# Four phase heads with only what is first needed in front, and prompt scores as two products of stacked halves, in a two-layer streaming encoder step

## What is computed

```
layer 0:  h = x @ w_in            -> MLA (latent attention, 8 heads) || retention (8 heads)
layer 1:  h = x @ w_in            -> GLA (gated linear attention)    || SWA (windowed softmax attention)
both:     x = LayerNorm(a*x + concat(parts) @ w_out);  x = LayerNorm(a*x + ConvFFN(x))

SWA, per query row of the prompt: 8 query heads in 2 groups over 2 key/value heads of size 64,
  s = q . k * 64**-0.5   over its own chunk of 64 rows and the 128 rows before it, masked elsewhere
  o = softmax([s, sink]) @ v
MLA for a stream: s = (q_abs . cached latent + q_pe . cached rotary key) * scale over 1024 cached rows
```

## Time and profile before

| | |
|---|---|
| median of 3 runs | 3093.89 us (3088.95 to 3095.7) |
| profiled execution, its own time | 3095.32 us |
| its span, first to last instruction | 3093.5 us |
| PE (TensorE) busy | 2939.1 us, 95% of the span |
| PE weight loads | 2612.2 us, 84% |
| DVE, ACT, POOL busy | 1648.3, 1056.4, 827.4 us: 53%, 34%, 27% |
| mean granted TensorE clock | 0.976 |
| instructions | 42586 |

### The profile page before, as it was taken

The page is one execution under the profiler, slowest core; times in us unless marked ns, Lnnn a source line. Parts: engine busy times, 40 slices in busy tenths (PEclk is TensorE's granted clock), DMA queues, the critical chain, the costliest instruction groups (busy, mean ns, idle before and its releaser), DMA issues. The chain is left out here.

```text
span 3093.5 us, 42586 instructions
## 1 busy us (share of the span) xinstructions
PE 2939.1 (95%) x15775; PEld 2612.2 (84%) x15775; DVE 1648.3 (53%) x2648; ACT 1056.4 (34%) x2087; POOL 827.4 (27%) x699
## 2 busy tenths in 40 slices
PE   8899789998999999999997998998999999999997
PEld 7455678886899999999996898996899999999996
DVE  3566635656545555555547442445455555555556
ACT  5334532333432322222333453333332232222323
POOL 1245211112232322222335000102233322222324
PEclk9999899999999999999998998998999999999998
DMA  3100531103111111111103101113111111111112
GB/s 126 34 8 13 180 117 35 35 22 128 46 55 41 41 45 43 41 41 41 41 28 107 47 5 40 39 35 121 35 60 41 41 47 41 47 41 41 41 35 80
DMA packets 72712, 162.57 MB, mean 53 GB/s; under 512 B 19514, under 2 KB 33995, under 8 KB 71540
## 3 DMA queue, kind: packets, MB, share of 16 engines
q1 hardware_dynamic: 72596, 161.00, 16.3%
HBM read 146.51 MB, written 15.11 MB: 52 GB/s over the span
## 5 line engine op out<-in xcount | busy, mean ns | idle before, releaser
L135 PE MATMUL psum<-xT_hi,tk_whi 128*128 128x384 f32 x2112 | 711.7, 337 | 7.5 <-ACT tk_u L2317 3.3
L136 PE MATMUL psum<-xT_lo,tk_whi 128*128 128x384 f32 x2112 | 710.5, 336 | 0.0
L137 PE MATMUL psum<-xT_hi,tk_wlo 128*128 128x384 f32 x2112 | 710.3, 336 | 0.0
L2516 DVE TENSOR_TENSOR x_or_mix<-x_or_mix,psum 128x512 f32<-128x512 f32 x684 | 465.9, 687 | 243.2 <-PE psum L137 242.8
L135 PEld LDWEIGHTS psum<-xT_hi,tk_whi 128*128 128x128 f32 x2112 | 397.5, 188 | 11.4 <-ACT tk_u L2320 6.1
L136 PEld LDWEIGHTS psum<-xT_lo,tk_whi 128*128 128x128 f32 x2112 | 397.5, 188 | 1.5
L137 PEld LDWEIGHTS psum<-xT_hi,tk_wlo 128*128 128x128 f32 x2112 | 397.6, 188 | 0.0
L2479 DVE SCALAR_TENSOR_TENSOR tk_c<-tk_u,tk_cw,tk_c 128x1168 f32<-128x1168 f32 x84 | 157.8, 1878 | 447.3 <-ACT tk_c L2328 447.3
L135 PE MATMUL psum<-tk_dhi,tk_gh 128*128 128x512 f32 x756 | 294.7, 390 | 1.7 <-ACT tk_u L2320 1.7
L137 PE MATMUL psum<-tk_dhi,tk_gl 128*128 128x512 f32 x756 | 295.0, 390 | 0.0
L136 PE MATMUL psum<-tk_dlo,tk_gh 128*128 128x512 f32 x756 | 294.9, 390 | 0.0
(11 more groups left out here) (395 smaller groups left out, 5475.2 us busy)
## 6 DMA issues: line engine op xcount, KB each, us to landing
tk_wraw<-in_w_up SPq DMA_DIRECT2D x88, 512.0 KB, 3.6
tk_draw<-in_w_down SPq DMA_DIRECT2D x44, 512.0 KB, 3.6
s_ckv<-in_c_ckv SPq DMA_DIRECT2D x8, 1024.0 KB, 6.2
retw_raw<-in_w_ret SPq DMA_DIRECT2D x32, 256.0 KB, 3.5
tk_mix_wraw<-in_w_out SPq DMA_DIRECT2D x16, 512.0 KB, 4.2
glaw_raw<-in_w_gla SPq DMA_DIRECT2D x32, 192.0 KB, 3.2
x_or_mix<-in_xT SPq DMA_DIRECT2D x9, 512.0 KB, 10.2
tk_xin<-in_x_in SPq DMA_DIRECT2D x9, 512.0 KB, 3.5
```

Of the source, the lines that this page charges most:

```text
L135: nc.tensor.matmul(out, a[0], b[0], start=first, stop=False)
L136: nc.tensor.matmul(out, a[0], b[1], start=False, stop=False)
L137: return nc.tensor.matmul(out, a[1], b[0], start=False, stop=last)
L2516: nc.vector.tensor_tensor(x, x, PS[:, down_bank(n), :], ALU.add).then_inc(ad, 1)
```

## The change

Five places, all in the order of work or in the form of operands; the results and all big products stay.

1. **MLA samples, stream 0.** ACT rounds pieces 0 and 1 first, then the queries, then the rotary keys, then pieces 2 and 3. DVE does the queries, pieces 0 and 1, the low halves of the queries, pieces 2 and 3, and the own mask last.
2. **Linear phases.** PE no longer waits for POOL's memsets at its start (at slot 2 now), ACT only for the one of the values; the others are cleared later. In retention POOL makes the low half of chunk 2 first and clears the values behind it. ACT runs Silu on one column first, so that the table is loaded there.
3. **SWA scores.** Operands of 128 rows in fp32r: Q1 holds the high half of q twice, K1 the high half of k over its low half; Q2 holds the low half of q over mask rows, K2 the high half of k over mask rows. Q1.K1 + Q2.K2 makes the scores of a head. They live in columns of `x_or_mix` that nothing uses then (`swa_halves`). ACT makes four copies of q instead of two and two of k instead of one; DVE makes the low halves (`halves_lo`), PE waits for them; POOL clears a staging buffer; SP loads mask rows twice more.
4. **SWA order.** In a slot with one step and a projection (`shared`), PE leaves the last two k chunks of the projection until the scores are issued; ACT's copy of v and DVE's rotation of that tile move behind.
5. **Mix head.** In layer 0 the as-is half of tile 0 no longer waits for the transposes. In both layers the high half of chunk 4 comes before `finish_stats`.

```diff
# MLA samples, ACT and DVE
+            act.wait_ge(kl[0], came(0, 0))
+            pieces_hi(0, PIECES[:2])
             q_hi(0, 0)
-            keys_hi(0, 0)
+            kpe_hi(0)
+            pieces_hi(0, PIECES[2:])
...
+            queries(0, 0)
+            keys_lo(0, 0, (0, 1))
+            queries_lo(0, 0)
+            keys_lo(0, 0, (2, 3))
             dve.wait_ge(ol_, 16)
             own_mask(0)
-            queries(0, 0)
-            queries_lo(0, 0)
-            keys_lo(0, 0)
# linear phases: SP, POOL, PE, ACT
-            sp.wait_ge(qz, 1)
+            sp.wait_ge(qz, 2)
...
-            nc.gpsimd.memset(S0[:], 0.0)
-            nc.gpsimd.memset(vz[:], 0.0)
+            if ret:
+                w.make_lo(pool, nc.gpsimd, 0, 0, (2,))
+            nc.gpsimd.memset(vz[:], 0.0).then_inc(vzd, 1)
+            if ret:
+                w.make_lo(pool, nc.gpsimd, 0, 0, range(4, KD, 2))
             nc.gpsimd.memset(QK[:], 0.0)
             if not ret:
                 nc.gpsimd.memset(Sc[:], 0.0)
             nc.gpsimd.memset(Qm[:], 0.0).then_inc(qz, 1)
-            if ret:
-                w.make_lo(pool, nc.gpsimd, 0, 0, range(2, KD, 2))
+            nc.gpsimd.memset(S0[:], 0.0).then_inc(qz, 1)
...
-            pe.wait_ge(qz, 1)
...
+                if s == 2:
+                    pe.wait_ge(qz, 2)
...
-            act.wait_ge(qz, 1)
             if ret:
                 make_hi(0, range(G.raw, KD))
+            act.wait_ge(wz, 1)
+            nc.scalar.activation(warm[:], warm[:], ACT.Silu)
+            act.wait_ge(vzd, 1)
# SWA: SP, POOL, PE, ACT, DVE
+            sp.wait_ge(on, 2)
+            sp.dma_start(Pb[HD:HD + 8, 0, :], A["swa_q_rows"][:, 0:1024]).then_inc(rwl, 16)
+            sp.dma_start(Pb[HD:HD + 8, 1, :], A["swa_k_rows"][:, 0:1024]).then_inc(rwl, 16)
...
+            nc.gpsimd.memset(Pb[:], 0.0).then_inc(on, 1)
...
+                    if n >= 2:
+                        pe.wait_ge(qkl, tiles_to(n - 1))
...
-                        keys = KT[0:HD + 4, max(t - 1, 0) * P:(t + 1) * P]
-                        last = nc.tensor.matmul(o[:, 0:P] if t == 0 else o, QT[0:HD + 4, slot(t), h, :], keys, start=True, stop=True,
-                                                skip_group_check=True)
+                        nc.tensor.matmul(o, Q1[:, *q], K1[:, near], start=True, stop=False, skip_group_check=True)
+                        last = nc.tensor.matmul(o, Q2[:, *q], K2[:, near], start=False, stop=True, skip_group_check=True)
...
-                    project(s, range(KD))
+                    project(s, range(KD - 2 if shared(s) else KD))
...
+                if rest is not None:
+                    project(rest, range(KD - 2, KD))
                 if m:
                     values(m - 1, n)
...
-                        nc.scalar.activation(QT[0:HD, slot(t), odd::2, :], src.rearrange("p (q n) -> p q n", q=2), ACT.Copy)
+                        for copy in range(2):
+                            nc.scalar.activation(Q1[64 * copy:64 * copy + 64, slot(t), :, odd, :], src.rearrange("p (q n) -> p q n", q=2), ACT.Copy)
...
+            def halves_lo(n):
+                i, t = where(n)
+                dve.wait_ge(qkT, n + 1)
+                for odd in range(2):
+                    own = slice(64 * odd, 64 * odd + 64)
+                    nc.vector.tensor_tensor(Q2[0:HD, slot(t), :, odd, :], PS[own, 2, 0:2 * P].rearrange("p (q n) -> p q n", q=2),
+                                            Q1[own, slot(t), :, odd, :].bitcast(F), ALU.subtract)
+                nc.vector.tensor_tensor(K1[HD:P, t, :], PS[0:64, 2, 2 * P:3 * P], K1[0:HD, t, :].bitcast(F), ALU.subtract).then_inc(qkl, 1)
...
+                if rest is not None:
+                    rotate(rest)
+                    if rest == TP:
+                        make_lo(1, (5, 7))
...
+                if 2 <= s <= TILES and where(s - 1)[1] != TP:
+                    halves_lo(s - 1)
# mix head: ACT (DVE's mix_lo likewise, with the waits asis and mh)
             def mix_hi(t):
-                act.wait_ge(mt, t + 1)
+                if t:
+                    act.wait_ge(mt, t + 1)
                 if AS_IS:
-                    nc.scalar.activation(xTh[:, 0:AS_IS, tile(t)], by_k(XM[:, t, 0:AS_IS * P]), ACT.Copy)
+                    last = nc.scalar.activation(xTh[:, 0:AS_IS, tile(t)], by_k(XM[:, t, 0:AS_IS * P]), ACT.Copy)
+                    if t == 0:
+                        last.then_inc(asis, 1)
+                if t == 0:
+                    act.wait_ge(mt, 1)
...
             m.make_hi(act, 3)
+            m.make_hi(act, 4)
             L.finish_stats()
-            m.make_hi(act, 4)
```

More of the change, by code:

```diff
@@ L813, in _, with pieces_hi, kpe_hi @@
         def _(act):
+            def pieces_hi(s, pieces):
+                for i in pieces:
+                    nc.scalar.activation(cacheH[s][i], cacheT[s][i], ACT.Copy).then_inc(chi, 1)
+            def kpe_hi(s):
+                nc.scalar.activation(k3[s], kraw[s][0:96, 0:PAST], ACT.Copy).then_inc(khi, 1)
             def keys_hi(b, s):
                 act.wait_ge(kl[s], came(b, s))
-                for i in PIECES:
-                    nc.scalar.activation(cacheH[s][i], cacheT[s][i], ACT.Copy).then_inc(chi, 1)
-                nc.scalar.activation(k3[s], kraw[s][0:96, 0:PAST], ACT.Copy).then_inc(khi, 1)
+                pieces_hi(s, PIECES)
+                kpe_hi(s)
             def q_hi(b, s):
@@ L868, in queries_lo, with keys_lo @@
                 nc.vector.tensor_tensor(q3[64:96, s], qpb[64:96, s, :], q3[64:96, s].bitcast(F), ALU.subtract).then_inc(qsp, 1)
-            def keys_lo(b, s):
-                for n, i in enumerate(PIECES):
+            def keys_lo(b, s, which=range(4)):
+                for n in which:
+                    i = PIECES[n]
                     dve.wait_ge(chi, 4 * b + n + 1)
@@ L1315, in _ @@
             out.norm_late = norm_late
+            nc.vector.memset(warm[:], 0.0).then_inc(wz, 1)
             nc.vector.memset(S[:, 0, :], 0.0).then_inc(sr, 1)
@@ L1380, in phase_swa @@
     (lg, lgk, ln, gt, su, suk, dsu, ach) = (c.sem("gate_" + s) for s in names)
+    qkl, rwl, rwr = (c.sem("swa_" + s) for s in ("qkT_lo", "rows_loaded", "rows_rounded"))
+    XMR = c.rounded("swa_halves", "x_or_mix", [P, NT, D])
+    K1, K2 = XMR[:, 0:TP, 0:P], XMR[:, 0:TP, P:2 * P]
+    Q1, Q2 = (XMR[:, 4 * x:4 * x + 4, 2 * P:4 * P].rearrange("p (s a) (b n) -> p s a b n", s=2, n=P) for x in range(2))
     SCALE = HD ** -0.5
@@ L1386, in phase_swa @@
     SLOTS = UNITS + 1
+    shared = lambda s: s < TILES and len(STEPS.get(s, ())) == 1
     where = lambda n: (n // NT, ORDER[n % NT])
@@ L1552, in values, with step @@
                 last.then_inc(pv, 1)
-            def step(m, n=None):
+            def step(m, n=None, rest=None):
                 if m:
@@ L1617, in _ @@
                 if steps:
-                    step(steps[-1], s - 3 if 3 <= s < 3 + NT else None)
+                    step(steps[-1], s - 3 if 3 <= s < 3 + NT else None, s if shared(s) else None)
                 if s == TILES:
@@ L1670, in step @@
                     nc.scalar.activation(PTs[:, (m - 1) % 2, 4:4 + nb, :], PS[:, 7, 0:nb * P].rearrange("p (b n) -> p b n", n=P), ACT.Copy).then_inc(pta, 1)
+                if rest is not None:
+                    keep_v(rest)
+                    if rest == TP:
+                        make_hi(1, range(4, KD))
                 if m < UNITS:
@@ L1705, in _ @@
                     make_hi(1, range(4))
-                if s < TILES:
+                if s < TILES and not shared(s):
                     keep_v(s)
@@ L1709, in _ @@
                     keep_qkT(s - 1)
-                if s == TP:
-                    make_hi(1, range(4, KD))
                 if steps:
-                    step(steps[-1])
+                    step(steps[-1], s if shared(s) else None)
                 gate(s)
@@ L1816, in _ @@
                     make_lo(1, (1, 3))
-                if s < TILES:
+                if s < TILES and not shared(s):
                     rotate(s)
-                if s == TP:
-                    make_lo(1, (5, 7))
                 if steps:
-                    step(steps[-1], s - 3 if 3 <= s < 3 + NT else None)
+                    step(steps[-1], s - 3 if 3 <= s < 3 + NT else None, s if shared(s) else None)
+                if 2 <= s <= TILES and where(s - 1)[1] != TP:
+                    halves_lo(s - 1)
                 if s == 15:
```

37 lines of the change are left out of this document (33 added, 4 removed).

## The result

The changed kernel takes 3070.0 us (median of 4 runs, 3066.4 to 3071.4) against 3094.2 before (4 runs): a ratio of 0.992, interval 0.9906 to 0.9934. In a later session it took 3070.2 against 3094.2, ratio 0.9922 (0.9909 to 0.9936). The forecast was 3070. The sum held. Of the terms under it one failed in kind, as the experiments show, and one in size, so that the exact hit is in part luck.

The account below looks back on a forecast made before the run. PE was taken as the bound, busy 2939.1 of 3093.5 us, with losses at phase heads, in SWA and in slow clock behind waits. Terms summed to -24.9 us from 3095.3, giving 3070 us; 8-in-10 range 3058 to 3082.

Parts of the forecast that it names:

- Part 1: MLA samples: ACT's pieces go before the queries, so PE starts earlier; -1.8 us, gain between 0 and 2.8.
- Part 2: Retention head: PE starts without POOL's memsets and chunk 6 comes sooner; -4.0 us, ends -2.5 and -5.5.
- the end that it gave to a shorter slow stretch: Retention head: -5.5 us if the clock falls less because the idle before PE's start shrinks.
- Part 3: GLA head: table loaded while POOL clears the values, PE starts at 1910.6; -3.1 us, ends -2.0 and -4.5.
- the 1.19 us from ACT to PE: GLA head: rest of the 2.47 us between ACT's and PE's starts after the table load, kept for the new start.
- Part 4: SWA scores stacked in fp32r: 0.78 us a unit, -10.9 us; +0.7 for one-tile units, +0.25 for the phase's head.
- The step of 0.122 us: SWA scores: time per fp32r matmul of 256 columns, from a line through wider products; upper end 0.176.
- The added work hides beside PE: SWA slots: extra ACT copies and DVE's `halves_lo` cost nothing; without that cover a slot pays up to 1.1 us.
- rival F: SWA gets a new ring of waits through PE, ACT and DVE, making the kernel slower: 3105 us, chance 0.02.
- Part 5: SWA order: no stall for DVE's weights copy at the seam, -5.0 us; shorter wait near the end, -1.
- Part 6: Mix heads: PE's wait for chunk 4 goes, POOL delays DVE's norm chain; -0.4 us layer 0, +0.4 layer 1.

Follow-up runs that it names:

- run 1: The changed kernel with the stacked SWA scores but the old order in a slot: 3089.0 us against 3091.0, ratio 0.9993.
- run 2: The kernel before with the new SWA order alone, scores in float32 as they were: 3082.8 us against 3091.0, ratio 0.9973.
- run 3: The changed kernel with the SWA phase of the kernel before: 3084.2 us against 3094.7, ratio 0.9964.
- run 10: The changed kernel, DVE making all mix low halves, GLA's norm-weight wait moved to first use, `halves_lo` before writing out in SWA's last two slots: 3051.7 us against 3094.2.

## Why the prediction was right, and where not

- **Part 1, samples, -1.8.** Right: -2.0 by the means of nine executions, 2.4 in the pair with fewer loads. DVE's piece did take 2.44 us beside POOL.
- **Part 2, retention, -4.0.** Right: -4.3 between the two profiles and -5.5 by the means, the end that it gave to a shorter slow stretch; the start and chunk 6 come earlier as it said.
- **Part 3, GLA, -3.1.** Mis-sized: -1.5. The step that failed is the 1.19 us from ACT to PE, taken from a head in which DVE's own wait for norm weights was already over. PE starts 3.4 to 4.2 us into the phase instead of the 2.8 of the step; with that wait away it starts at 2.2, and the phase gains 4.1, part of it by the clock.
- **Part 4, scores.** The step of 0.122 us was right (0.12), and so was 0.75 a unit in the steady slots. "The added work hides beside PE" failed in kind. It was argued from busy shares, 4.03 of 10.11 us for ACT; but it is not the share that matters, it is ACT's place in the chain transposes, q and k, attention weights, values. I had put the price of losing that cover at up to 1.1 us a slot; the waits are 0.5 to 1.2, but the slow clock behind them was in no term. Without the moved matmuls the form costs 10 us (run 1); with them it gives 4 to 7 instead of 10.0 (10.9 less 0.7 and 0.25), the rest going to `halves_lo` in the last slots and to slots that other work bounds. My rival F feared a ring through ACT and DVE and had the wrong wait: what came late was the copy of the attention weights, and it came late only without the order.
- **Part 5, order, -5.0 and -1.** Right at the seam: -5.6 with the order alone (run 2 against run 3). It is DVE's new order that does it, as forecast: its copy of the weights starts 1.51 us into the seam's slot in run 2, where it started 5.40 us into it in run 3, behind the split. I gave it no worth in steady slots, and there it has none by itself, but it is the cover on which part 4 rests. At the end nothing is won for certain; what the clock does there is larger than the term.
- **Part 6, mix, 0.0.** Right in sum, with the wrong operation named: DVE's chunk 1 in three executions of seven, in the one of the other four that is shown POOL's own chunk 4 and DVE's L1309, L1290 (now L1310) in neither.
- **The sum.** By the means of all executions of old and new code the phases give -2.0 - 5.5 - 0.3 - 15.3 - 1.5 - 0.9 = -25.5 us, of which the old SWA's 217.9 carries 4; the medians give -24.2. It came out at 3070 because form and order were made together, as forecast together, and to the microsecond by luck: what part 4 and GLA lacked was made up for by the clock at SWA's end and by retention. Alone, the form would have been forecast 10 us faster, and it is 10 slower.

## What to carry to other kernels

- Before work is added to an engine that is half idle, look where that engine stands in the chain that the bound engine waits for next; independent work moved into just that gap of the bound engine is what pays for it, so make the two edits as one.
- Where two engines block each other, count the slower one's instruction in the other's chain before you give it a share. Here DVE with POOL's chunks 4 and 6 as well brought the second tile 2.5 to 4.4 us earlier in each mix head. Whether POOL should then keep chunks 0 and 2 stays open: run 10, in which DVE has all eight, changed other things too.
- When a wait is removed, list all that the next engine in the chain waits for, also the loads whose arrival was hidden.
- Price what a short new wait does to the clock behind it: in run 1 waits of 0.5 to 0.7 us came with a lower clock in two slots of five, and those were 1.3 and 2.2 us longer than the old ones.

## What the hardware showed that I had not expected

- **The clock of one and the same code.** The slow stretches move between executions: with the same instructions and the same waits SWA's old end took 44.9 us in one and 37.3 in another, and the unchanged first 323 us of the program 322.2 to 328.3. Phases must be compared over several traces.
- **A product of 128 by 128 with 256 columns in fp32r** steps at 0.12 us, each with weights of its own (L1564 and L1565 after), and one in float32 of 68 rows with as many columns costs two of 0.22 (L1527 before).
- **Two engines 0.05 us apart:** POOL's instruction began at 709.41, DVE's at 709.46, and it cost DVE 2.2 us. In four other executions of this code POOL began 0.2 to 0.4 us behind DVE and took 3.02 to 3.26 us itself, and the third tile came 0.6 to 1.6 us sooner than where DVE had lost. The same code does not always win the same race.
